# A gather queue on GpSimd: which picks wait for TensorE, and how many picks stand between the row fetches

## The chip, the cores and the metric

The kernel runs on one core of one Trainium2 chip. The metric is device time in microseconds. The kernel before has a median of 2885.0 us over three timed runs (2873.63 to 2889.99).

## The reference

One encoder layer over 1024 tokens of width 1024. A mixer sub-layer (gated linear attention and pooling) comes first; the change does not touch it. The channel sub-layer is a product-key retrieval: 8 heads choose 16 of 16384 single-neuron experts each, so 128 experts per token.

```python
def peer_ffn(h, w_q, sub_keys, u_tab, v_tab):
    q = (ht @ w_q).reshape(T, PEER_HEADS, 2, PEER_HALF)
    s = jnp.einsum('thpd,hpnd->thpn', q, sub_keys)
    vals, idx = lax.top_k(s, K)
    cand = vals[:, :, 0, :, None] + vals[:, :, 1, None, :]
    top_s, top_pos = lax.top_k(cand.reshape(T, PEER_HEADS, K * K), K)
    ...
    experts = (i1 * PEER_NKEYS + i2).reshape(T, PEER_HEADS * K)
    gates = jax.nn.softmax(top_s, axis=-1).reshape(T, PEER_HEADS * K)
    def block(args):
        a = jax.nn.gelu(jnp.einsum('td,ted->te', xb, u_tab[eb]), approximate=False)
        coeff = (gb * a.astype(jnp.float32)).astype(xb.dtype)
        return jnp.einsum('te,ted->td', coeff, v_tab[eb])
```

## The kernel before, in words

The first 1175 us hold the mixer, the queries, the scores and the first of two sweeps over the key table u. In a sweep the table is walked in 128 tiles of 128 experts (the tile number m is called a position below):

- the first key pass (m = 0 to 127) computes gelu(u . h) of every expert for the first 3 blocks of 128 tokens,
- the second key pass (m = 128 to 255) computes it for the other 5 blocks; a tile is 48 matmuls on TensorE (L1470), and every third tile is followed by 8 small ones that build the dense gates (L1964),
- the value pass (m = 256 to 383) walks the table v and adds coefficient times value row for the last 4 token blocks as a dense product; a tile is 24 matmuls of 128x512 (L1982).

The first 4 token blocks are not summed densely but gathered, on the side, during the second key pass and the value pass. For each of their 4 x 128 = 512 columns e (one chosen expert for each of 128 tokens) there are three steps:

1. a **pick**: an indirect DMA that GpSimd issues (`pick_act`, L1907), which fetches one activation per token into a column of `picked_act`,
2. a **row**: an indirect DMA that GpSimd issues (`fetch_row`, L1914), which fetches 128 rows of v, 4 KB each, into one of 7 buffers `rows`,
3. the multiply-add `ys <- rows, coef, ys` on VectorE (`add_row`, L1818). Before every eighth row VectorE forms 8 coefficients (L1809), for which the 8 picks of that group (a turn) must have landed.

GpSimd does nothing else there: its program is one fixed list of picks and rows. The order comes from `picks_by(e)`, the number of picks issued before row e. Before the change it is 13 + e, so 13 picks are ahead of row 0 and then one pick stands between two rows until all 512 are out. The list is paced: `pace(position)` makes GpSimd wait for TensorE to reach a position (through the semaphore `beats`, three marks per tile, or `tile_done`). Row e is held to `row_issue(e)`, which is 1.5 tiles ahead of where VectorE uses it in the second key pass; the pick before it has a pace of its own, half a row spacing earlier. From position 253.5 on (`2 * N - LEAD[1]`) nothing is paced any more; a row then waits only for its buffer (`rows_done`, seven rows back).

VectorE's program is in step with the tiles. At step m it does, in this order, the coefficient product of tile m + 2 (L1845, `cf`), the low half of the table tile m + 2 (`lo`, L108), the low half of the coefficients of m + 1 (`c_lo`, also named `free_hi_r`, L108), gates and top-k, and then the rows from `rows_by(m - 1)` to `rows_by(m)`: 12 rows per 5 tiles in the second key pass, 12 per 7 in the value pass. The engine works in program order, so a row that is late holds up the `lo` and `c_lo` behind it, and TensorE waits for those with `lo_ready` and `clo_ready`. In the second key pass TensorE needs from step m the `lo` of a tile two ahead; in the value pass it also needs the `c_lo` of the next tile. Rows 290 and 291 are the last of step 254; rows 292 to 294 are those of step 255. Tile 256, the first of the value pass, needs the `c_lo` of step 255, which comes behind row 291.

Of the kernel before, what the change touches and what calls it, by code (L numbers as in the profile page):

```python
# [35 lines left out]
N = NKEYS  # L36
CHOSEN = HEADS * TOPK
# [4 lines left out]
GATHERED = 4  # L42
# [33 lines left out]
POOL_ADDS = 2  # L76
ROWS_FROM, PICKS, BEATS = 133, 4, 4
ROW_EVERY = (5 / 12, 7 / 12)
PICKS_FROM, PICKS_AHEAD = N + 0.75, 12
LEAD = (1.5, 2.5)  # L80


# [1215 lines left out]
def gate_stores(s, block):  # L1298

    return len([n for n in range(block) if gate_buffer(2 * n) == s])  # L1300
# [18 lines left out]
def rows_by(m):  # L1319

    if m < ROWS_FROM:
        return 0
    late = 2 * N - 1
    rows = 12 * (min(m, late) - ROWS_FROM + 1) // 5
    return min(GATHERED * CHOSEN, rows + max(0, m - late) * 12 // 7)


def row_issue(e):

    key_rows = rows_by(2 * N - 1)  # L1330
    if e < key_rows:
        return ROWS_FROM + e * ROW_EVERY[0] - LEAD[0]
    return max(row_issue(key_rows - 1), 2 * N + (e - key_rows) * ROW_EVERY[1] - LEAD[1])


def picks_by(e):

    return min(GATHERED * CHOSEN, PICKS_AHEAD + e + 1) if e >= 0 else 0


def last_row_at(s):
# [548 lines left out]
def sweeps_gpsimd(g, pool):  # L1890

    v_table = g.i["v"].rearrange("n p d -> (n p) d")
    act_tables = [a.rearrange("n p s -> (n p s)").unsqueeze(1) for a in (g.act_early, g.act_late)]
    index = lambda a, e: a[:, e // CHOSEN, e % CHOSEN:e % CHOSEN + 1]

    def act_complete(last):
        for s in range(GELUS):
            pool.wait_ge(g.act_stored[s], 16 * ((last - s) // GELUS + 1))

    def pick_act(e):  # L1900
        turn = e // TURN
        if e == EARLY * CHOSEN:
            act_complete(2 * N - 1)
            pool.wait_ge(g.chosen_ready, 2)
        if turn >= PICKS and e % TURN == 0:
            pool.wait_ge(g.picked_in[turn % PICKS], 16 * TURN * (turn // PICKS))
        pool.indirect_dma_start(out=g.picked_act[:, e:e + 1], out_offset=None, in_=act_tables[e // (EARLY * CHOSEN)],  # L1907
                                in_offset=bass.IndirectOffsetOnAxis(ap=index(g.aidx, e), axis=0))\
            .then_inc(g.picked_in[turn % PICKS], 16)

    def fetch_row(e):
        if e >= ROWS:
            pool.wait_ge(g.rows_done, e - ROWS + 1)
        pool.indirect_dma_start(out=g.rows[e % ROWS][:], out_offset=None, in_=v_table,  # L1914
                                in_offset=bass.IndirectOffsetOnAxis(ap=index(g.eidx, e), axis=0))\
            .then_inc(g.rows_in[e % ROWS], 16)

    def pace(position):
        if position >= 2 * N - LEAD[1]:
            return  # L1920
        tile, beat = divmod(int(BEATS * min(position, 3 * N - 1)), BEATS)
        if beat:
            pool.wait_ge(g.beats, (BEATS - 1) * (tile - N) + beat)
        else:
            pool.wait_ge(g.tile_done, tile)

    pool.wait_ge(g.chosen_ready, 1)
    act_complete(N - 1)
    for e in range(GATHERED * CHOSEN):
        for p in range(picks_by(e - 1), picks_by(e)):  # L1930
            pace(PICKS_FROM + p * ROW_EVERY[0] / 2 if e == 0 else row_issue(e) - ROW_EVERY[e >= rows_by(2 * N - 1)] / 2)
            pick_act(p)
        if e == 0:
            for s in range(2):
                pool.wait_ge(g.gate_stored[s], 16 * gate_stores(s, EARLY_BLOCKS))
            pool.wait_ge(g.gate_ps, EARLY_BATCHES)
        pace(row_issue(e))
        fetch_row(e)
    for q, t in enumerate(DENSE_ORDER[:POOL_ADDS]):
        pool.wait_ge(g.y_scaled, q + 1)  # L1940
        pool.wait_ge(g.x1_dense_in, 16 * DENSE)
        pool.tensor_tensor(g.y[t][:], g.y[t][:], g.x1_dense[t][:], ALU.add).then_inc(g.y_added, 1)
# [75 lines left out]
def experts(g):  # L2018
# [3 lines left out]
    with nc.psum_tensor("sps_all", [P, 2, TT, NKEYS], F32) as sps_all, nc.Block() as block:  # L2022
# [24 lines left out]
        @block.gpsimd  # L2047
        def _(pool):
            sweeps_gpsimd(g, pool)
# [62 lines left out]
```

## Time and profile before

| | us |
|---|---|
| median of 3 timed runs | 2885.0 |
| the profiled execution, its own time | 2853.14 |
| its span, first to last instruction | 2851.3 |
| second key pass, 128 tiles | 1175 to 2114.9 |
| value pass, 128 tiles | 2114.9 to 2842.0 |

The profiled execution is shorter than all three timed ones. The mean granted TensorE clock in it is 0.997 of full. Over the span TensorE is busy 98%, VectorE 76%, ScalarE 44% and GpSimd 47%; GpSimd's share is small because it has almost nothing to do in the first 1180 us. A view lists the start and the length of a piece of work and, in brackets, how long the engine stood idle before it and what ended that.

### The profile page before, as it was taken

How to read it: one execution, taken by the hardware profiler on the slowest of the kernel's cores; microseconds unless marked ns; L12 is line 12 of the kernel's file. 1: busy time of each engine (PE TensorE's matmuls, PEld its weight loads, DVE VectorE, ACT ScalarE, POOL GpSimd, SP SyncE). 2: the span in 40 equal slices, each digit the busy share in tenths (PEclk: the TensorE clock that was granted, in tenths of full speed). 3: DMA queues.
4: the chain of work that ended last, by engine and by line, in shares of the span. 5: the costliest groups of instructions: out<-in, count | busy, mean ns of one | idle time of the engine just before them, and what ended most of it. 6: DMA issues, size and time to landing. Idle time of an engine off the chain costs nothing.

```text
span 2851.3 us, 43778 instructions
## 1 busy us (share of the span) xinstructions
PE 2783.6 (98%) x16074; PEld 2544.2 (89%) x16074; DVE 2159.0 (76%) x3706; ACT 1250.7 (44%) x2302; POOL 1341.6 (47%) x1039
## 2 busy tenths in 40 slices
PE   7998999999999999999999999999999999999998
PEld 6786788889999999999999999999997777787777
DVE  7646546887668778688888888777767877887788
ACT  4334552233367767644455535444522323232323
POOL 0002000000000000377888887777788888888884
PEclk9999999999999999999999999999999999999999
DMA  6520222225556556589898988988999999999997
GB/s 279 227 73 31 104 105 79 67 96 181 182 185 214 189 202 210 190 306 316 303 312 309 309 317 315 318 304 312 329 371 356 352 339 333 368 343 350 326 351 270
DMA packets 328418, 721.39 MB, mean 253 GB/s; under 512 B 44000, under 2 KB 159840, under 8 KB 326368
## 3 DMA queue, kind: packets, MB, share of 16 engines
q1 hardware_dynamic: 238176, 451.18, 44.9%
q0 software_dynamic: 90112, 268.76, 27.1%
q8 instruction: 47, 0.77, 0.1%
q14 instruction: 83, 0.68, 0.1%
HBM read 605.50 MB, written 114.30 MB: 252 GB/s over the span
## 4 chain that ended last, share of the span: by engine, by line
PE 56%; POOL 18%; issue 5%; DVE 2%; ACT 2%; DMA 1%; DVEq 0%; SPq 0%; ACTq 0%; POOLq 0%
PE mix L1470 44%; POOL picked_act L1907 9%; POOL rows L1914 9%; PE mix L118 5%; PE sps_all L1982 2%; PE mix L1982 2%; PE sps_all L1964 2%; DMA rows<-in_v,eidx 1%; ACT onehot L1677 1%; PE sps_all L1557 1%; DVE lo L108 0%; DVE onehot L1759 0%; DMA wq_raw<-in_w_q 0%; DVEq L1159 0%; ACT hi L103 0%
## 5 line engine op out<-in xcount | busy, mean ns | idle before, releaser
L1907 POOL DMA_INDIRECT picked_act<-act_early,aidx x384 | 491.2, 1279 | 1032.2 <-PE mix L1470 926.4
L1470 PE MATMUL mix<-a_hi,hi 128*128 128x320 f32 (+1 forms) x3072 | 809.7, 318 | 2.0 <-DVE lo L108 2.0
L1818 DVE SCALAR_TENSOR_TENSOR ys<-rows,coef,ys 128x1024 f32<-128x1024 f32 x504 | 638.4, 1286 | 228.4 <-DMA rows<-in_v,eidx 203.3
L1470 PE MATMUL mix<-a_lo,hi 128*128 128x320 f32 (+1 forms) x3072 | 808.9, 317 | 0.0
L1470 PE MATMUL mix<-a_hi,lo 128*128 128x320 f32 (+1 forms) x3072 | 808.8, 317 | 0.0
L1914 POOL DMA_INDIRECT rows<-in_v,eidx x512 | 650.9, 1271 | 164.0 <-issue 139.6
L108 DVE TENSOR_TENSOR lo<-raw,hi 128x1024 fp32r<-128x1024 f32 x384 | 468.8, 1221 | 208.8 <-ACT hi L103 208.6
L1470 PEld LDWEIGHTS mix<-a_hi,hi 128*128 128x128 f32 x3072 | 533.8, 188 | 3.3 <-ACT gelu L1686 2.3
L1470 PEld LDWEIGHTS mix<-a_hi,lo 128*128 128x128 f32 x3072 | 534.7, 188 | 0.0
L1470 PEld LDWEIGHTS mix<-a_lo,hi 128*128 128x128 f32 x3072 | 534.6, 188 | 0.0
L103 ACT ACTIVATE hi<-raw 128x1024 fp32r<-128x1024 f32 x384 | 404.7, 1054 | 290.7 <-PE mix L1982 278.9
L1689 ACT ACTIVATE gelu<-mix 128x640 f32<-128x640 f32 x128 | 90.2, 705 | 464.6 <-PE mix L1470 464.5
L1982 PE MATMUL sps_all<-hi,free_hi_r 128*128 128x512 f32 x680 | 198.4, 393 | 10.8 <-DVE free_hi_r L108 10.5
L1982 PE MATMUL mix<-hi,free_hi_r 128*128 128x512 f32 x680 | 195.5, 389 | 0.0
L1907 POOL DMA_INDIRECT picked_act<-act_late,aidx x128 | 170.9, 1335 | 39.0 <-issue 39.0
L1982 PEld LDWEIGHTS sps_all<-hi,free_hi_r 128*128 128x128 f32 x680 | 125.7, 188 | 44.9 <-DVE free_hi_r L108 19.6
L1686 ACT ACTIVATE gelu<-mix 128x384 f32<-128x384 f32 x128 | 62.8, 491 | 202.2 <-PE mix L1470 202.0
L1982 PEld LDWEIGHTS mix<-hi,free_hi_r 128*128 128x128 f32 x680 | 127.7, 188 | 26.5
L103 ACT ACTIVATE free_hi_r<-cf 128x512 fp32r<-128x512 f32 x85 | 53.6, 631 | 146.5 <-DVE cf L1845 146.3
L1982 PE MATMUL sps_all<-lo,free_hi_r 128*128 128x512 f32 x340 | 105.1, 390 | 0.0
L1982 PE MATMUL mix<-lo,free_hi_r 128*128 128x512 f32 x340 | 104.7, 389 | 0.0
L1677 ACT ACTIVATE free_hi_r<-free_hi_r,gate_hi 128x128 fp32r<-128x128 f32 x304 | 92.8, 392 | 26.6 <-DVE free_hi_r L1759 26.6
(274 smaller groups left out, 3865.0 us busy)
## 6 DMA issues: line engine op xcount, KB each, us to landing
raw<-in_u SPq DMA_DIRECT2D x256, 512.0 KB, 5.0
raw<-in_v SPq DMA_DIRECT2D x128, 512.0 KB, 5.6
act_late<-gelu SPq DMA_DIRECT2D x128, 320.0 KB, 4.7
act_in<-act_late SPq DMA_DIRECT2D x128, 256.0 KB, 6.1
act_early<-gelu SPq DMA_DIRECT2D x128, 192.0 KB, 1.8
gate_d<-free_lo SPq DMA_DIRECT2D x19, 1024.0 KB, 6.2
gt<-gate_d SPq DMA_DIRECT2D x64, 256.0 KB, 7.3
free_lo<-gate_d SPq DMA_DIRECT2D x64, 256.0 KB, 7.4
```

The source lines that it names most:

```text
L103: return act.activation(hi, raw, ACT.Copy)
L108: return dve.tensor_tensor(lo, raw, hi.bitcast(F32), ALU.subtract)
L118: done = pe.matmul(acc[:, cols], w, a[:, k, cols], start=first, stop=last)
L1470: done = pe.matmul(dst, w, a[:, k, cols], start=first, stop=last)
L1677: last = act.activation(onehot[:, t, part * NKEYS:(part + 1) * NKEYS], onehot[:, t, NKEYS:].bitcast(F32), ACT.Copy, scale=gate[:, first + ...
L1686: act.activation(g.gelu[m % GELUS][:, 0:EARLY * P], g.mps[m % 2][:, 0:EARLY * P], ACT.Gelu).then_inc(g.gelu_done, 1)
L1689: act.activation(g.gelu[m % GELUS][:].rearrange("p (a b) -> p a b", b=wide), g.mps[m % 2][:].rearrange("p (a b) -> p a b", b=HALF)[:, :, 0 ...
L1818: dve.scalar_tensor_tensor(sums, row, coef, sums, ALU.mult, ALU.add).then_inc(g.rows_done, 1)
L1907: pool.indirect_dma_start(out=g.picked_act[:, e:e + 1], out_offset=None, in_=act_tables[e // (EARLY * CHOSEN)], in_offset=bass.IndirectOff ...
L1914: pool.indirect_dma_start(out=g.rows[e % ROWS][:], out_offset=None, in_=v_table, in_offset=bass.IndirectOffsetOnAxis(ap=index(g.eidx, e), ...
L1964: last = pe.matmul(g.gps[:, t], g.onehot_1[u][:, t, :], g.onehot_2[u][:, t, :], start=True, stop=True)
L1982: done = pe.matmul(g.yps[t][:, cols], c, v[:, cols], start=n == 0 and k == 0, stop=n == N - 1 and k == 2)
```

## The change

Two things in one function and its caller: `picks_by` spreads the picks otherwise, and picks behind row 0 are no longer paced.

```diff
-PICKS_FROM, PICKS_AHEAD = N + 0.75, 12
+PICKS_FROM, PICKS_AHEAD, MORE_PICKS = N + 0.75, 12, 24
...
 def picks_by(e):
 
-    return min(GATHERED * CHOSEN, PICKS_AHEAD + e + 1) if e >= 0 else 0
+    last_key = rows_by(2 * N - 1) - 1
+    if e < 0:
+        return 0
+    if e <= last_key:
+        return PICKS_AHEAD + 1 + e + e * MORE_PICKS // last_key
+    return min(GATHERED * CHOSEN, picks_by(last_key) + (e - last_key) * 7 // 8)
...
         for p in range(picks_by(e - 1), picks_by(e)):
-            pace(PICKS_FROM + p * ROW_EVERY[0] / 2 if e == 0 else row_issue(e) - ROW_EVERY[e >= rows_by(2 * N - 1)] / 2)
+            if e == 0:
+                pace(PICKS_FROM + p * ROW_EVERY[0] / 2)
             pick_act(p)
```

`last_key` is 294: 295 rows belong to the second key pass. By the new rule 13 picks are ahead of row 0 as before, 328 are ahead of row 292 (305 before), 331 ahead of row 294 (307 before), 507 ahead of row 496 (509 before), and the last pick stands ahead of row 501 (499 before). The total is 512 picks and 512 rows in both. No other engine's list of work changes.

GpSimd in the second key pass, rows 10 to 13. Here L1907 is a pick and L1914 a row, with the semaphores that each waits for. Before:

```order
L1907 DMA picked_act<-act_early,aidx 128x1 [waits beats]
L1914 DMA rows_3624<-in_v,eidx 128x1024 [waits rows_done,beats]
L1907 DMA picked_act<-act_early,aidx 128x1 [waits beats]
L1914 DMA rows_3625<-in_v,eidx 128x1024 [waits rows_done,tile_done]
L1907 DMA picked_act<-act_early,aidx 128x1 [waits beats]
L1914 DMA rows_3626<-in_v,eidx 128x1024 [waits rows_done,beats]
L1907 DMA picked_act<-act_early,aidx 128x1 [waits beats]
L1914 DMA rows_3627<-in_v,eidx 128x1024 [waits rows_done,beats]
```

The same place now, where L1912 is a pick and L1919 a row:

```order
L1912 DMA picked_act<-act_early,aidx 128x1
L1919 DMA rows_3624<-in_v,eidx 128x1024 [waits rows_done,beats]
L1912 DMA picked_act<-act_early,aidx 128x1
L1919 DMA rows_3625<-in_v,eidx 128x1024 [waits rows_done,tile_done]
L1912 DMA picked_act<-act_early,aidx 128x1
L1919 DMA rows_3626<-in_v,eidx 128x1024 [waits rows_done,beats]
L1912 DMA picked_act<-act_early,aidx 128x1 x2
L1919 DMA rows_3627<-in_v,eidx 128x1024 [waits rows_done,beats]
```

The picks have lost their waits for TensorE's marks, the rows have kept theirs, and a second pick stands ahead of row 13; this repeats at every twelfth or thirteenth row.

GpSimd early in the value pass, rows 300 to 304. Before there is a pick between any two rows:

```order
L1914 DMA rows_3627<-in_v,eidx 128x1024 [waits rows_done]
L1907 DMA picked_act<-act_early,aidx 128x1 [waits picked_in3]
L1914 DMA rows_3621<-in_v,eidx 128x1024 [waits rows_done]
L1907 DMA picked_act<-act_early,aidx 128x1
L1914 DMA rows_3622<-in_v,eidx 128x1024 [waits rows_done]
```

And now, with one gap in every eight rows:

```order
L1912 DMA picked_act<-act_early,aidx 128x1 [waits picked_in3]
L1919 DMA rows_3623<-in_v,eidx 128x1024 [waits rows_done]
L1919 DMA rows_3624<-in_v,eidx 128x1024 [waits rows_done]
L1912 DMA picked_act<-act_early,aidx 128x1
L1919 DMA rows_3625<-in_v,eidx 128x1024 [waits rows_done]
L1912 DMA picked_act<-act_early,aidx 128x1
```

One pick in eight is missing here, since it has been issued in the second key pass.

## Rows read from the trace of the kernel before

**Rows 1.** Stretches: us, busy of PE PEld DVE ACT POOL (count), clock, DMA share, GB/s.

```profile
1175.00:2115.00 940.00, 938.80 (x6458) 938.54 (x6457) 760.13 (x1067) 439.23 (x920) 743.81 (x605) 1.00 0.89 311
2115.00:2842.00 727.00, 707.62 (x3073) 574.62 (x3071) 581.77 (x636) 219.75 (x270) 570.13 (x421) 1.00 0.95 341
```

**Rows 2.** Chain of waits, key tiles, then value tiles (start us, us, what).

```profile
2035.69 0.96 PE sps_all L1964 x8
2036.65 21.12 PE mix L1470 x144
...
2722.11 2.72 PE sps_all L1982 x12
```

**Rows 3.** The same for the inner part of the two passes.

```profile
1260.00:2100.00 840.00, 838.80 (x5772) 838.54 (x5771) 684.83 (x921) 392.50 (x822) 673.98 (x545) 1.00 0.91 315
2120.00:2780.00 660.00, 640.65 (x2779) 519.51 (x2778) 526.08 (x576) 196.83 (x236) 539.36 (x396) 1.00 0.97 347
```

**Rows 4.** Waits of GpSimd, 1260 to 2790 (total us, times, longest us).

```profile
POOL picked_act L1907 <- issue: 133.8, 439, 0.3
POOL rows L1914 <- issue: 132.6, 435, 0.3
POOL rows L1914 <- PE mix L1470: 10.4, 34, 0.3
POOL picked_act L1907 <- PE mix L1470: 9.8, 32, 0.3
```

**Rows 5.** Picks and rows: duration min/median/max in ns, first and last start.

```profile
L1907 POOL DMA_INDIRECT picked_act<-act_early,aidx x384: 942/1022/3235, 1181.5 to 2365.7; - x192
...
L1914 POOL DMA_INDIRECT rows<-in_v,eidx x512: 941/1083/3232, 1201.7 to 2814.0; - x171
```

**Rows 6.** Timeline of GpSimd, 1236 to 1253 (start, us, what, idle before).

```profile
1244.03 1.44 POOL L1914 DMA_INDIRECT rows<-in_v,eidx  x1 [1.88 <-PE mix L1470]
...
1252.18 1.24 POOL L1914 DMA_INDIRECT rows<-in_v,eidx  x1 [2.06 <-DVE ys L1818]
```

**Rows 7.** Waits of VectorE in the second key pass, then the value pass.

```profile
DVE ys L1818 <- DMA rows<-in_v,eidx: 85.2, 60, 4.0
...
DVE ys L1818 <- DMA rows<-in_v,eidx: 118.1, 98, 4.2
```

**Rows 8.** Waits of TensorE's weight loads in the value pass.

```profile
PEld sps_all L1982 <- DVE free_hi_r L108: 19.6, 24, 2.0
PEld sps_all L1982 <- DVE c_lo L108: 13.4, 12, 2.5
```

**Rows 9.** Timelines of GpSimd, VectorE and TensorE around the first value tile.

```profile
2103.93 1.09 POOL L1914 DMA_INDIRECT rows<-in_v,eidx  x1 [0.30 <-issue]
...
2108.67 1.28 DVE L1818 SCALAR_TENSOR_TENSOR ys<-rows,coef,ys 128x1024 f32<-128x1024 f32 x1 [0.28 <-DMA rows<-in_v,eidx]
2109.87 0.69 DVE L1845 TENSOR_TENSOR cf<-gt,act_in 128x512 f32<-128x512 f32 x1
2110.47 1.22 DVE L108 TENSOR_TENSOR lo<-raw,hi 128x1024 fp32r<-128x1024 f32 x1
2111.61 0.68 DVE L108 TENSOR_TENSOR c_lo<-cf,c_hi 128x512 fp32r<-128x512 f32 x1
...
2114.89 0.63 PE L1982 MATMUL sps_all<-hi,c_hi 128*128 128x512 f32 x2
```

**Rows 10.** Chain, VectorE and TensorE at TensorE's last stop for a row; last matmuls.

```profile
2703.36 6.59 DMA rows<-in_v,eidx
...
2708.58 1.28 DVE L1818 SCALAR_TENSOR_TENSOR ys<-rows,coef,ys 128x1024 f32<-128x1024 f32 x1 [2.24 <-DMA rows<-in_v,eidx]
...
2714.76 0.76 PE L1982 MATMUL sps_all<-hi,c_hi 128*128 128x512 f32 x2 [2.08 <-DVE c_lo L108]
...
2841.36 0.61 PE L1982 MATMUL mix<-hi,free_hi_r 128*128 128x512 f32 x2
```

**Rows 11.** GB/s moved in 40 slices of the span.

```profile
GB/s 279 227 73 31 104 105 79 67 96 181 182 185 214 189 202 210 190 306 316 303 312 309 309 317 315 318 304 312 329 371 356 352 339 333 368 343 350 326 351 270
```

## The prediction

> **What bounds the kernel now.** I read first the stretches by pass, then the chain of waits, then GpSimd's waits, then the timelines where the passes meet. In the second key pass TensorE is busy 938.8 of 940 us [rows 1]: the pass is TensorE's own time. The chain shows three tiles in 21.12 us and the 8 gate matmuls in 0.96 us [rows 2], so 22.08 us per three tiles, 7.36 us each. In the value pass 12 matmuls take 2.72 us [rows 2], a tile of 24 takes 5.44 us, and 128 tiles would take 696.3 us. The pass takes 727 [rows 1]: 30.7 us are lost in it. TensorE's weight loads wait there 33.0 us in 36 pieces, all for VectorE's low halves [rows 8]; those halves stand in program order behind `ys`, and VectorE waits 118.1 us for rows to land, 98 times [rows 7]. In the second key pass it also waits for rows, 85.2 us in 60 pieces, but nobody feels it [rows 1, 7].
>
> Who makes the rows late? GpSimd's share of 80% looks like slack and is none. From 1260 to 2100 it issues 545 DMAs, one per 1.541 us; from 2120 to 2780 it issues 396, one per 1.667 us [rows 3]. Between any two of them stand 0.3 us, and no single wait from 1260 to 2790 is longer: all 439 and 435 "issue" pieces are 0.3, and so are those put down to TensorE, 10.4 us in 34 and 9.8 us in 32 pieces [rows 4], which is 0.3 us each again. So the queue runs without a stop; the marks that picks and rows are held to have already gone by when it reaches them. The shortest pick and the shortest row take 0.94 us [rows 5], 1.25 us with the gap. The second key pass asks for 12 picks and 12 rows per 5 tiles, 4.8 DMAs or 7.40 us of GpSimd per 7.36 us tile; the value pass asks for 24 per 7 tiles, 3.43 DMAs or 5.71 us of GpSimd per 5.44 us tile. The first pass is level, the second is GpSimd's. The picks moved are to even this out.
>
> **Picks without their pace.** This removes waits that last nothing. Only near the start are there real ones: 1.88 us less the usual 0.3 for TensorE ahead of the row at 1244.0, and 2.06 less 0.3 for a `ys` ahead of the row at 1252.2 [rows 6], 3.3 us in all; the former is a row's own pace and stays in the code. What can be won is that more work is done before them. By row 16 one more pick has gone out (the first comes ahead of row 13), so I take 1.5 us won, between 0 and 3.3. Of the rest of this edit I take 0.
>
> **The picks that come earlier, in the second key pass.** By `picks_by`, 328 picks stand ahead of row 292 now and 305 before: 23 more. What one costs has no row of its own: issues last from 0.94 us up to 3.2 us, with medians of 1.02 and 1.08 [rows 5]. From below: it costs the shortest issue, 1.25 us [rows 5], if the time above that (1.541 - 1.25 = 0.29 us on average) is tied to what VectorE does meanwhile, of which there is no more per tile than before; 23 x 1.25 = 28.8 us. From above: the average of the stretch, 23 x 1.541 = 35.4 us. Nothing reasonable lies below zero here, as GpSimd has no idle time to put them in. Whether the time above the shortest issue follows VectorE's work, the trace doesn't say. The Trainium skill has a rule on it: its page "SBUF — State Buffer" (Who interferes with whom) says that a DMA issued by GpSimd stalls while a VectorE instruction holds the port pair that the two engines share, and that a `tensor_tensor` does not hold the part that writing descriptors needs. By the first half the low end would hold, by the second the high end, since most of VectorE's work here has two inputs like a `tensor_tensor`; no row here separates the two.
>
> I take 32 us, the middle. Rows are then late by 32 - 1.5 = 30.5 us where the passes meet. What does TensorE have to spare there? Row 292 goes out at 2103.93. The last row of step 254 is done by 2109.95 (2108.67 + 1.28); behind it come `cf`, `lo` and `c_lo`, done at 2112.29; tile 256 starts at 2114.89 [rows 9]. Its `c_lo` was ready 2.6 us early. So tile 256 starts 30.5 - 2.6 = 28 us later, near 2143 (bounds: 28.8 - 3.3 - 2.6 = 23 and 35.4 - 2.6 = 33). Most of that comes as stops of TensorE in the last third of the key pass: until the lag has used up the two-tile lead of `lo`, there is nothing to see.
>
> Behind the late rows on VectorE stand `lo`, the one-hot comparisons of the gates and top-k, and behind `lo` SP's next table load. All of them are held up by the same delay and not by one each; I cost them at nothing beyond it.
>
> **The picks that are gone from the value pass.** The last stop of TensorE for a row is at 2714.76: 2.08 us, for a `c_lo` that was behind the row issued at 2703.36 [rows 10], which is row 472 by count. From there TensorE runs to 2842.0 at its own speed. From row 292 to row 472 are 180 rows, 105 tiles, and 599.4 us. Before there are 180 picks between them, 360 DMAs at 1.665 us; now 486 - 328 = 158 picks, 338 DMAs. That is 338 x 1.665 = 562.8 us, or with the low price of a pick 599.4 - 22 x 1.25 = 571.9 us: 5.36 to 5.45 us of GpSimd per tile, against TensorE's 5.44. GpSimd is just level with TensorE, so of the 30.7 us of stops most go, and single ones stay, since the length of an issue varies from 0.94 to 3.2 us [rows 5]. I take 5 us left (0 to 15). Saved: 26 us.
>
> The sum is 28 - 26 = +2 us: 2855 us on the profiled execution's 2853.1.
>
> There is a second way to the same number, and it is the one that I trust. Ahead of row 472 stand 485 picks before and 486 now, and 472 rows in both. GpSimd never stops, so it reaches row 472 at the same time within one pick (+1.3 to +1.7) and the 1.5 us won at the start. If TensorE still waits for a row thereabouts, the end is where it was. If it doesn't, the end is set by the start of the value pass: 2143 + 696.3 = 2839, within 2834 and 2844, against 2842.0. The end is the later of the two, and with both so near each other a little more: 0 to +4. The change moves the loss from one pass to the other; it takes no work from the queue that sets the pace.
>
> The timed runs before lie 31.9 us above the profiled execution, 1.1%. Nothing shown says where. I carry the difference over unscaled: 2885 + 2 = 2887 us.
>
> **Rivals.**
> - *The value pass doesn't give the time back* (slower). TensorE's stops there would come from the transfers. For it: the pass moves 341 GB/s with the DMA engines at 0.95 [rows 1], and at 5.44 us a tile that would have to be 341 x 727 / 696 = 356 GB/s; most slices of the pass are below that. Against it: the slices also hold one of 368 GB/s in the pass and one of 371 where the passes meet [rows 11], and the row that TensorE last stopped for landed 6.59 us behind its issue [rows 10]: it was the issue that was late. Price: the key pass pays 28 us, the value pass gives between nothing and half, so +14 to +28, about +20: 2905 us. It decides where the transfers can't keep 356 GB/s over the whole pass. The Trainium skill gives such a limit: "DMA: Bandwidth & Descriptors" (Where 436 GB/s comes from) puts HBM at about 358 GB/s per core. By that page the value pass could just reach its 356 GB/s, with nothing over for unevenness. The trace's slice of 371 speaks against a limit below that.
> - *The key pass has room* (faster). In the profile GpSimd is level with TensorE (7.40 to 7.36 us). If in the timed runs the 31.9 us extra are mostly TensorE's or VectorE's, GpSimd would have up to that much room before the passes meet, would be held by its paces, and the 23 early picks would cost little there while the value pass still gives 26. It would be -15 to -26, about -20: 2865 us. Against it: nothing in the profile shows such room; the waits of 0.3 us say the opposite.
> - *The change doesn't do what it says*: the free picks have no idle time to go into. That is part of my forecast for the pace; for the order of picks it isn't so, since the list is fixed by the program.
>
> **How the numbers follow.** The forecast has 60%, the slower rival 23%, the faster one 14%; the other 3% I leave open. Within 0.5% (14 us) is what a measurement of this kernel can't tell from no change. My own terms leave it only at their far ends: 33 us in the key pass and 15 left in the value pass give +17, 23 and 0 give -8. So of the 60, 54 are same, 4 slower, 2 faster; of the rivals, 4 of the 23 and 3 of the 14 fall inside 0.5%. With the rest split this gives faster 0.14, same 0.62, slower 0.24. The likeliest case alone reaches from 2877 to 2902; with the rivals, and the spread of 16 us that the runs before show, the range is 2866 to 2909.
>
> **What would show it.** In the profile after: GpSimd's waits from 1260 to 2790 still all 0.3 us; the DMAs issued per us in either pass as before; TensorE with stops of 20 to 30 us in the last third of the second key pass, with VectorE's `lo` (or the one-hots) as what it waits for; the first value tile near 2143; a value pass of about 701 us instead of 727, and VectorE's waits for rows there well below 118 us. I am wrong if tile 256 starts before 2130 (the key pass had room, or a pick costs less than the shortest issue), if GpSimd shows waits of over 0.3 us for TensorE along the key pass, or if the value pass stays above 715 us with GpSimd no longer late.

## The result, and the profile after

The changed kernel took 2892.84 us, the median of 22 runs (2879.96 to 2915.84), against 2878.62 us for the kernel before (22 runs, 2869.20 to 2891.15, the three shown above among them): a ratio of 1.0051, interval 1.0037 to 1.0065. The forecast was 2887 us and +2, within 2866 to 2909; the time is within its range, and the difference is +14.

The profiled execution took 2892.82 us, at the median of the timed runs; that of the kernel before took 2853.14, below all of its own. So of the 39.7 us between the two traces about 26 are not shown by the timed runs, which differ by 14.

The stretches by pass after the change, with the columns of [rows 1]:

```profile
1176.00:2184.00 1008.00, 971.79 (x6456) 956.64 (x6455) 759.21 (x1068) 440.55 (x920) 752.50 (x635) 0.98 0.86 292
2184.00:2880.00 696.00, 696.00 (x3073) 576.40 (x3072) 580.28 (x636) 208.20 (x268) 542.15 (x391) 1.00 0.97 353
```

Against [rows 1] the key pass is 68 us longer, where 28 were forecast, and the value pass 31 us shorter, without any stop of TensorE. The key pass has lost in two columns: 36 us in which TensorE is idle, and a clock of 0.98 (2% of 1008 us is 20 us).

What ended the idle time of TensorE's weight loads in the key pass, then the same for VectorE and its rows (engine, what, releaser: total us, times, longest us):

```profile
PEld mix L1475 <- issue: 48.0, 77, 1.9
PEld sps_all L1970 <- issue: 2.2, 5, 0.5
```

```profile
DVE ys L1823 <- DMA rows<-in_v,eidx: 7.7, 8, 2.6
```

This is not what was forecast. The stops stand inside key tiles, in 77 short pieces, and wait for nothing that the profile shows; and VectorE waits 7.7 us for rows where it waited 85.2 [rows 7]. TensorE's timeline at the first of them (start us, us, what, idle before):

```profile
1299.16 0.31 PE L1475 MATMUL mix<-a_lo,hi 128*128 128x320 f32 x1
1300.03 0.40 PE L1475 MATMUL mix<-a_lo,hi 128*128 128x320 f32 x1 [0.56 <-issue]
1300.74 0.31 PE L1475 MATMUL mix<-a_hi,lo 128*128 128x320 f32 x1 [0.31 <-issue]
1301.46 0.30 PE L1475 MATMUL mix<-a_hi,lo 128*128 128x320 f32 x1 [0.41 <-issue]
1302.87 0.45 PE L1475 MATMUL mix<-a_hi,hi 128*128 128x320 f32 x2 [1.10 <-issue]
```

Matmuls that elsewhere follow one another every 0.15 us come 0.7 to 1.4 us apart, one by one, in the middle of a tile whose operands are all there. Two windows of TensorE (us, busy and count, clock, DMA share, GB/s), one over such an episode and one between two of them:

```profile
1480.00:1495.00 15.00, 10.95 (x50) 0.66 0.86 280
1502.00:1545.00 43.00, 43.00 (x298) 1.00 0.85 294
```

There are some 15 such episodes from 1300 to 2168 (pieces less than 12 us apart taken as one), none in the value pass. Beside or behind eight of them the clock is granted at 0.5, the 1.2 GHz level, for 3.4 to 10.2 us: 44.4 us in all, which costs 22. With the 36 us of idle time that is 58 of the 68 us. The other 10 are in the busy column too, since a matmul that stands alone counts 0.3 to 0.4 us where one in a row takes 0.15. GpSimd, in the meantime (1260 to 2720), had time over:

```profile
POOL picked_act L1912 <- issue: 135.3, 444, 0.3
POOL rows L1919 <- issue: 118.9, 390, 0.3
POOL rows L1919 <- remote: 33.6, 20, 2.7
POOL rows L1919 <- DVE ys L1823: 18.7, 15, 4.0
POOL rows L1919 <- PE mix L1475: 17.7, 24, 1.8
```

Three groups of waits are longer than the 0.3 us of [rows 4]: GpSimd is held by TensorE's marks, by `ys`, and by something that the profile doesn't name (`remote`). TensorE lost its time first and thereby gave the queue the room that it lacks in the trace before. So this trace can't show what the moved picks cost. It took experiments.

### The profile page after: what moved, and what is told of

It reads as the page before. It is cut to its first block, busy times and chain, and to the rows that moved or that the text cites. A ratio compares the mean times of both kernels' runs of the same rounds, so it can differ in the third digit from the quotient of the medians.

```text
span 2891.0 us, 43743 instructions
## 1 busy us (share of the span) xinstructions
PE 2807.3 (97%) x16074; PEld 2566.0 (89%) x16074; DVE 2157.3 (75%) x3706; ACT 1241.4 (43%) x2302; POOL 1322.8 (46%) x1039
## 3 DMA queue, kind: packets, MB, share of 16 engines
q1 hardware_dynamic: 238176, 451.18, 44.4%
q0 software_dynamic: 90112, 268.76, 27.2%
## 4 chain that ended last, share of the span: by engine, by line
PE 80%; DVE 2%; issue 2%; ACT 1%; DVEq 0%; DMA 0%; SPq 0%; ACTq 0%
PE mix L1475 48%; PE sps_all L1988 12%; PE mix L1988 12%; PE mix L118 5%; PE sps_all L1970 2%; ACT onehot L1682 1%; PE sps_all L1562 1%; DVE lo L108 0%; DVE onehot L1764 0%; DMA wq_raw<-in_w_q 0%; DVEq L1159 0%; ACT hi L103 0%; DVE rows L1887 0%; DVE idx L1178 0%; DVE idx L1167 0%
## 5 line engine op out<-in xcount | busy, mean ns | idle before, releaser
L1912 POOL DMA_INDIRECT picked_act<-act_early,aidx x384 | 474.0, 1234 | 1032.9 <-PE mix L1475 914.6
L1475 PE MATMUL mix<-a_lo,hi 128*128 128x320 f32 (+1 forms) x3072 | 819.6, 320 | 14.1 <-issue 14.0
L1475 PE MATMUL mix<-a_hi,hi 128*128 128x320 f32 (+1 forms) x3072 | 818.4, 320 | 13.0 <-issue 10.7
L1475 PE MATMUL mix<-a_hi,lo 128*128 128x320 f32 (+1 forms) x3072 | 817.1, 320 | 9.9 <-issue 9.6
L1919 POOL DMA_INDIRECT rows<-in_v,eidx x512 | 644.1, 1258 | 219.9 <-issue 136.5
L1823 DVE SCALAR_TENSOR_TENSOR ys<-rows,coef,ys 128x1024 f32<-128x1024 f32 x504 | 628.1, 1283 | 13.8 <-DMA rows<-in_v,eidx 7.7
L1475 PEld LDWEIGHTS mix<-a_lo,hi 128*128 128x128 f32 x3072 | 541.2, 190 | 21.3 <-issue 20.9
L1475 PEld LDWEIGHTS mix<-a_hi,lo 128*128 128x128 f32 x3072 | 540.7, 190 | 12.2 <-issue 12.1
L1912 POOL DMA_INDIRECT picked_act<-act_late,aidx x128 | 176.1, 1376 | 39.0 <-issue 39.0
L1682 ACT ACTIVATE free_hi_r<-free_hi_r,gate_hi 128x128 fp32r<-128x128 f32 x304 | 93.0, 394 | 1.4 <-DVE free_hi_r L1764 1.3
```

The lines of the kernel that those rows point to most:

```text
L1475: done = pe.matmul(dst, w, a[:, k, cols], start=first, stop=last)
L1682: last = act.activation(onehot[:, t, part * NKEYS:(part + 1) * NKEYS], onehot[:, t, NKEYS:].bitcast(F32), ACT.Copy, scale=gate[:, first + ...
L1823: dve.scalar_tensor_tensor(sums, row, coef, sums, ALU.mult, ALU.add).then_inc(g.rows_done, 1)
```

## The experiments

They ran in three sets on two other chips (called the other chips below), where the kernel before takes 2842 to 2844 us (2841.83, 2843.66 and 2842.08 in the sets, 19 to 28 runs each). The first and the third set are of one chip; the second (`more_48`, `more_12`, `half_picks`, `early_rows`) is of the other and holds no profile of the two kernels unedited. A ratio is to the kernel before in the same set. No profile there shows an episode inside a tile.

**The kernel before and the kernel after, unedited**, each profiled twice (the second pair in the last set, to see how far two executions of one kernel differ).

> The kernel before, profiled once more. Theory Q (the queue: TensorE loses time only to late rows): a second key pass of 940 us with no stop of TensorE inside a tile, a value pass of about 727 us, 2853 us in all. Theory S (TensorE starves inside tiles of the second key pass, in episodes that no wait explains, each followed by a stretch at the lower clock; the first profile of the kernel before happened to hold none): a second key pass of 955 to 990 us with such episodes, and a value pass nearer 700 us since GpSimd catches up during them; about 2875 us, the level of the other timed runs of this kernel.

> The changed kernel, once more, timed in five rounds. Both theories: ratio 1.003 to 1.007. Theory Q: a second key pass of about 968 us and a value pass of about 700 us. Theory S: a second key pass of 990 to 1015 us, of which all above 940 us stands in pauses inside tiles and in halved clock after them; value pass 697 us.

> The kernel before, one more look, for the stops of TensorE inside tiles that no wait explains (15 episodes in the first profile of the changed kernel, none in the two profiles of this one). If they belong to the chip and not to the change, and this is the chip on which the kernel before takes about 2880 us, they are here too: clock below 0.993 and a second key pass above 955 us. On a chip where it takes about 2842 us: none, 939 and 720 us.

> The changed kernel, one more look, for the same stops. On a chip where the kernel before takes about 2842 us: no episodes inside tiles, key pass 955 to 960 us, value pass 697 to 706 us. On the one where it takes about 2880 us: episodes again, key pass about 1000 us. If there are episodes here and none in the look at the kernel before, they go with the change (theory S2).

Measured: before 2843.51 and 2842.44 in the two profiled executions; after 2848.18 over its timed runs (the profiled one 2851.48), 1.0028 [1.0012, 1.0045], and 2846.47 in the second look. Stretches by pass, before (two looks), then after (two looks):

```profile
1175.40:2114.10 938.70, 938.55 (x6457) 938.29 (x6456) 759.11 (x1067) 439.05 (x920) 741.42 (x609) 1.00 0.90 312
2114.10:2832.40 718.30, 704.68 (x3073) 575.63 (x3072) 583.86 (x637) 217.52 (x270) 562.75 (x417) 1.00 0.96 344
```

```profile
2118.50:2831.30 712.80, 702.16 (x3074) 574.78 (x3072) 582.40 (x636) 217.56 (x270) 558.96 (x415) 1.00 0.96 345
```

```profile
1176.80:2134.00 957.20, 946.00 (x6457) 942.84 (x6455) 758.30 (x1066) 438.75 (x920) 756.58 (x625) 0.99 0.88 305
2134.00:2839.00 705.00, 699.03 (x3072) 578.29 (x3072) 583.10 (x638) 208.44 (x269) 550.87 (x401) 1.00 0.97 352
```

```profile
1178.10:2137.70 959.60, 944.06 (x6457) 940.81 (x6456) 760.75 (x1067) 438.66 (x920) 757.72 (x629) 1.00 0.88 305
2137.70:2834.20 696.50, 696.48 (x3073) 576.36 (x3072) 582.60 (x636) 212.21 (x270) 548.16 (x397) 1.00 0.97 355
```

This is the trade that was forecast, smaller on both sides: the key pass gives 18.5 to 19.6 us, the value pass gets 13 to 16 back. Behind the value pass the span is another 1.2 to 1.4 us longer (10.7 and 10.5 us, against 9.3 twice before). GpSimd's waits in the first look after the change, from 1260 to row 472 at 2694:

```profile
POOL picked_act L1912 <- issue: 137.2, 450, 0.3
POOL rows L1919 <- issue: 129.2, 424, 0.3
POOL rows L1919 <- PE mix L1475: 7.0, 23, 0.3
```

Not one is longer than 0.3, nor in the second look. Row 472 goes out at 2694.0 and 2693.9 after the change, at 2694.4 and 2690.3 before it. What ended TensorE's stops (weight loads), and what the one-hots waited for on ScalarE, key pass:

```profile
PEld sps_all L1970 <- issue: 8.6, 8, 2.7
PEld mix L1475 <- DVE lo L108: 4.1, 2, 3.8
...
ACT free_hi_r L1682 <- DVE free_hi_r L1764: 122.9, 24, 7.7
```

The gate matmuls, which follow every third tile, are where the late rows show first: VectorE's comparisons (L1764) stand behind `ys`, ScalarE's weighing (L1682) behind them, the gate matmuls (L1970) behind that. Before the change ScalarE waits there for 23.6 and 32.3 us in the two looks, in 7 and 8 pieces.

Where the passes meet, TensorE and VectorE of the same trace:

```profile
2133.94 0.69 PE L1988 MATMUL sps_all<-hi,c_hi 128*128 128x512 f32 x2
...
2141.91 1.28 DVE L1823 SCALAR_TENSOR_TENSOR ys<-rows,coef,ys 128x1024 f32<-128x1024 f32 x1 [5.65 <-DMA rows<-in_v,eidx]
...
2144.86 0.68 DVE L108 TENSOR_TENSOR free_hi_r<-cf,free_hi_r 128x512 fp32r<-128x512 f32 x1
...
2145.59 1.22 PE L1988 MATMUL sps_all<-hi,free_hi_r 128*128 128x512 f32 x2 [5.97 <-DVE free_hi_r L108]
```

One row, 5.65 us late, holds `ys`, behind it `cf` and the low half, and TensorE for 5.97 us in its second value tile. After that it doesn't stop again. The row is row 294, and the last of the 24 early picks stands right ahead of it: from row 293 GpSimd goes through two picks, and row 294 goes out 8.0 us behind row 292, against 5.0 in both looks before. In the second look after it is 7.1 us, the row lands three us earlier, and TensorE has no stop there at all.

**The two halves apart.** The picks without their pace, in the old order; and the new order with the pace restored:

```diff
# unpaced_only, on the kernel before
-            pace(PICKS_FROM + p * ROW_EVERY[0] / 2 if e == 0 else row_issue(e) - ...)
+            if e == 0:
+                pace(PICKS_FROM + p * ROW_EVERY[0] / 2)
# order_only, on the kernel after: the reverse of this
```

> Only the pace of the picks behind row 0 is taken away; the order of picks and rows is that of the kernel before. Theory Q: nothing was waited for, so ratio 1.000 (within 0.002), at most 1.5 us faster. Theory S1 (picks without their waits bring the episodes): ratio 1.005, as the whole change, more episodes in the second key pass than the kernel before has, value pass 697 to 727 us.

> Only the new order of picks (24 more in the second key pass, seven per eight rows in the value pass); each pick keeps its pace. Theory Q: the same as the whole change, 1.005, since the waits were empty. Theory S1: ratio 1.000 or below, few episodes. Theory S2 (more picks in the second key pass bring the episodes, waits or not): 1.005.

Measured: unpaced_only 2846.7 us, 1.0019 [1.0004, 1.0034]; order_only 2848.22 us, 1.0024 [1.0007, 1.0041]. The key pass of each:

```profile
1182.20:2120.50 938.30, 938.30 (x6457) 938.30 (x6456) 759.27 (x1068) 439.50 (x920) 740.46 (x610) 1.00 0.91 313
```

```profile
1177.80:2138.40 960.60, 945.20 (x6456) 941.93 (x6455) 759.11 (x1066) 438.93 (x920) 759.37 (x627) 0.99 0.88 304
```

The order alone brings 20.6 to 21.9 us in the key pass, the pace none of it. By their times the two halves can't be told apart. The interval of unpaced_only just excludes 1.0000, and its trace doesn't show why: the passes take 938.3 and 712.9 us, as before, and the 3.7 to 6.8 us by which it is late are there at the start of the key pass (1182.2, against 1175.4 and 1178.5), ahead of the edit. That its 1.0019 is a loss by the pace is not shown.

**The dose.** Twice and half as many early picks, the value pass relaxed to match:

```diff
# more_48, on the kernel after
-... MORE_PICKS = N + 0.75, 12, 24
+... MORE_PICKS = N + 0.75, 12, 48
-    ... + (e - last_key) * 7 // 8)
+    ... + (e - last_key) * 6 // 8)
# more_12: 12, and * 15 // 16
```

> Twice the dose: 48 picks more in the second key pass instead of 24, and six picks per eight rows after it; no pace on the picks. 47 picks more than before stand ahead of row 292, 3 more ahead of row 472. Theory Q with the low price (a moved pick costs the shortest issue, 1.25 us): row 292 goes out 57 us later than before, the first value tile starts 48 us later (+30 over the changed kernel), the key pass is 987 to 995 us with halved clock after each stop, the value pass is 696 us with no stop at all; ratio 1.010 to 1.013. With the high price (1.54 us) row 292 is 72 us late and the ratio 1.016 to 1.018. Theory W (only what TensorE waits for counts, and the one-hots are no nearer to their limit than now): ratio 1.003, as now.

> Half the dose: 12 picks more in the second key pass and fifteen per sixteen rows after it; no pace on the picks. 11 picks more than before ahead of row 292, none more ahead of row 472. Theory Q: row 292 is 12 us late, which the room of VectorE where the passes meet takes up for the most part: key pass 939 to 945 us, value pass 710 to 715 us; row 472 goes out when it did, so ratio 1.000 to 1.002. Theory W (it pays to move some picks, and 24 were too many): 0.997.

Measured: more_48 2871.6 us, 1.0085 [1.0054, 1.0116]; more_12 2843.1 us, 0.9999 [0.9981, 1.0017]. By pass, more_48:

```profile
1179.40:2156.40 977.00, 948.50 (x6457) 943.86 (x6455) 759.02 (x1065) 440.82 (x923) 771.34 (x648) 0.99 0.87 299
2156.40:2862.20 705.80, 701.12 (x3072) 579.53 (x3072) 584.23 (x638) 206.42 (x267) 513.76 (x378) 0.99 0.97 351
```

Its key pass is 37 to 38 us longer than before, its value pass only 7 to 12 us shorter. No trace has a value pass below 696.0, and the picks moved beyond what that takes win nothing: GpSimd now waits 59.1 us in it for `ys` to free a row's buffer. The 9 us above 696.5 are one stop of 4.68 us at its start and the lower clock. So the loss grows with the picks moved (0.9999, 1.0028, 1.0085), and it does so on chips that show no stops inside tiles. The profile of more_12 (2850.6 us of span, 953.8 us in the key pass) is 9 us over its own median once the 1.8 us around the span are added; it shows stops in the key pass that its expectation did not have.

**Without half of the picks.** Every second pick is left out, with its data (the activations that it would bring stay at zero):

```diff
# half_picks, on the kernel before
 def pick_act(e):
+    if e % 2: return
...
-    wait_ge(picked_in, 16 * TURN * ...)
+    wait_ge(picked_in, 16 * TURN // 2 * ...)
```

> Leaves out every second pick (the columns stay zero, so the gathered sums lack half their terms); rows, order and paces as before. 768 issues on GpSimd instead of 1024. Theory Q: the queue has room and is held by its paces, the stops of TensorE in the value pass go (22 to 31 us): key pass 939 us, value pass 696 to 698 us, GpSimd with waits of over 0.3 us for TensorE all along; ratio 0.990 to 0.992. Rival T (the transfers bound the value pass): it stays above 710 us, since the bytes are the same.

Measured: 2826.4 us, 0.9932 [0.9911, 0.9953]. Its stretches, and GpSimd's waits from 1260 to 2790:

```profile
1176.20:2114.50 938.30, 938.30 (x6457) 938.30 (x6456) 755.04 (x1068) 438.73 (x920) 562.07 (x456) 1.00 0.90 313
2114.50:2811.00 696.50, 696.48 (x3073) 576.38 (x3072) 581.38 (x636) 208.66 (x270) 426.98 (x314) 1.00 0.97 353
```

```profile
POOL rows L1917 <- DVE ys L1819: 211.9, 106, 4.8
POOL rows L1917 <- PE mix L1470: 174.9, 121, 4.4
```

With GpSimd's load reduced it waits for its marks and for `ys`, as it hardly ever does before, and TensorE runs both passes without a stop. So what the queue costs the kernel before is about these 19 us, in the value pass. That no order of picks can win more follows if TensorE's own time stays as it is; it was not tested otherwise.

**Rows earlier.** The first row a tile earlier, all rows of the key pass due a tile earlier, and no pace on any pick; with 0, 24 and 12 early picks:

```diff
# early_rows on the kernel before; early_24 and early_12 on after and more_12
-ROWS_FROM, PICKS, BEATS = 133, 4, 4
+ROWS_FROM, PICKS, BEATS = 132, 4, 4
-LEAD = (1.5, 2.5)
+LEAD = (2.5, 2.5)
-            pace(...)          # before pick_act(p)
```

> The order of before, no pace on any pick (the first 13 included), rows from tile 132 instead of 133 and paced 2.5 tiles ahead instead of 1.5: the queue starts its rows 4 us earlier and loses none of the 5.6 us that it stands still before 1253. Theory Q: everything behind is 8 to 10 us earlier in the queue, so row 472 too, and the end by as much, since TensorE still waits for rows in the value pass: key pass 939, value pass 708 to 712 us, ratio 0.997. Theory W: the start is far from where TensorE waits, ratio 1.000.

> The changed kernel's order of picks, with the early start of the rows (rows from tile 132, paced 2.5 tiles ahead, no pick paced). The early start put row 292 12 us earlier after the start of the second key pass, the new order puts it 27 us later: 15 us in all. Theory Q: VectorE's room takes 9 of these, so the stops and halved clock of the second key pass fall from 18 us to 5 to 8, the value pass runs at TensorE's pace (697 to 700 us): ratio 0.994 to 0.996, faster than the kernel before and than the changed one. Theory W (moving picks earlier is bad whatever the start): 1.002.

> The same early start with half the dose of early picks (12, then fifteen per sixteen rows). Theory Q: row 292 about where it was before, no stop of TensorE in the second key pass, 939 us; the value pass keeps some stops (705 to 709 us against 718): ratio 0.995 to 0.997. Theory W: 1.000.

Measured: early_rows 2839.9 us, 0.9983 [0.9967, 0.9999]; early_24 2846.86 us, 1.0013 [1.0000, 1.0027]; early_12 2833.93 us, 0.9964 [0.9950, 0.9979]. The stretches of early_12, and TensorE at its one long stop:

```profile
1177.10:2124.70 947.60, 941.17 (x6456) 940.91 (x6456) 761.74 (x1071) 439.15 (x920) 749.42 (x625) 0.99 0.90 311
2124.70:2821.20 696.50, 696.50 (x3074) 576.88 (x3072) 578.54 (x633) 208.79 (x270) 536.75 (x401) 1.00 0.96 352
```

```profile
1623.76 2.07 PE L1968 MATMUL sps_all<-free_hi_r 128*128 128x256 f32 x8 [6.43 <-ACT free_hi_r L1682]
```

early_12 is faster than both kernels. The queue starts earlier and half as many picks are moved: the value pass runs at 696.5, and the key pass loses 8 to 9 us in place of 19. The early start alone (early_rows, 0.9983) does little: row 472 goes out at 2688.7, 2 to 6 us earlier than in the two looks at the kernel before, and the value pass still takes 713.9. What is left in early_12 is nearly all at one place, 6.43 us for the weighed one-hots ahead of the gate matmuls in tile 188, and the slower clock behind it (10.2 us). early_24 is a miss: 0.994 to 0.996 was expected. Its profiled execution, 2832.73 us, is the lowest of its 12 runs (up to 2853.35) and shows what was expected, 947.1 and 697.4 us by pass, so that one trace must not be read as the kernel. Why the other runs are slower is open.

## Why the prediction was right, and where it wasn't

*What was luck.* The time fell within the range on the first chips, but the one trace of the change there doesn't show the forecast's mechanism. It shows one of its signs of being wrong, GpSimd waiting for TensorE along the key pass, 17.7 us in pieces of up to 1.8. The +14 there is at the far end of what the forecast's own terms give (+17), and the stops that made most of that trace's loss were in no term. What bears the mechanism out is the other chips, where the measured difference is +6.

*The queue never stops: right on the other chips.* All waits of GpSimd in the stretch stay at 0.3 us, and row 472 goes out at the same time as before within the spread of two looks (2693.9 and 2694.0 to 2690.3 and 2694.4). The loss moved from one pass to the other, as the second way to the number had it.

*Unpaced picks worth 1.5 us (0 to 3.3): no gain in time.* In unpaced_only's trace row 292 goes out 919.1 us behind the first key tile, against 922.5 and 920.9, which is about the size forecast and hardly more than two looks differ; its timed runs gain nothing.

*23 picks ahead of row 292 cost 32 us: too much.* From the first tile of the key pass to row 292 it takes 922.5 and 920.9 us before, and 949.6, 947.3 and 949.9 in after_again, after_again_2 and order_only: 27.2 us more on average, 1.18 us a pick. That is a little under the low end of 1.25, not the middle. 47 picks in more_48 took 48.7 us more, 1.04 each; the 11 in more_12's single trace took 23.8, 2.2 each, so that one trace of such a kernel is not enough to price a pick (both are of the chip without a profile of the kernel before, and are held against the looks on the other). The mean per DMA from the pass's start to row 292 fell from 1.545 and 1.543 us before (597 DMAs) to 1.532 and 1.528 after (620) and 1.507 in more_48 (644). So a moved pick costs about the shortest issue, and the time above it doesn't grow with the number of picks. Of the Trainium skill's rule in "SBUF — State Buffer" (Who interferes with whom), weighed in the prediction, this speaks for the first half, that a GpSimd DMA is stretched by VectorE's work. It does not show it: no run here changed VectorE's work alone.

*Tile 256 28 us later: 19 to 20, and once 25 with the stop behind it.* After against before, the key pass is 18.5 us longer in the first pair, and TensorE then stops 5.97 us in tile 257; in the second pair it is 19.6 us longer, and no stop follows. Row 292 is 27.1 and 26.4 us late in its pass, so 8.6 and 6.8 us of that were taken up, where the forecast allowed 2.6. The 2.6 are right for the trace they were read from. On the other chips the queue was further ahead before the change, with row 292 at 922.5 and 920.9 us of the pass instead of 928.9, and VectorE stood still there for the high half of a table tile (9.10 and 7.02 us) and not for rows.

*"TensorE stops in the last third of the key pass": wrong place.* The step left out that the one-hots of the gates stand in the same queue on VectorE and are due after every third tile, with ScalarE's weighing still to come behind them. In both looks TensorE stops from tile 176 on (the pass is tiles 128 to 255), with 8 of the 23 early picks out, and for these one-hots first. The trace before the change has one such stop already, 1.2 us at 1748. In after_again_2:

```profile
1530.47 1.21 PE L1970 MATMUL sps_all<-free_hi_r 128*128 128x256 f32 x8 [0.48 <-ACT free_hi_r L1682]
```

The first long stop of after_again, at tile 188, waits for the low half behind them:

```profile
1624.48 0.56 PE L1475 MATMUL mix<-a_hi,hi 128*128 128x320 f32 x2 [3.56 <-DVE lo L108]
```

"I cost them at nothing beyond it" was said of just these comparisons.

*The clock: a term that the sum lacked.* Behind that stop of 3.56 us, and around and behind the one of 5.97 us, stands a stretch at the lower clock. Windows of after_again, with full clock in between (us, busy and count of PE, PEld, DVE, ACT, POOL, clock, DMA share, GB/s):

```profile
1625.10:1628.50 3.40, 3.40 (x15) 3.40 (x14) 3.33 (x7) 0.56 (x1) 2.78 (x3) 0.50 1.00 396
1640.00:1660.00 20.00, 20.00 (x140) 20.00 (x139) 16.11 (x30) 9.76 (x21) 15.51 (x14) 1.00 0.84 288
2143.90:2150.70 6.80, 5.11 (x12) 4.04 (x13) 6.76 (x9) 2.14 (x3) 5.58 (x5) 0.50 1.05 398
```

In that trace the 1.2 GHz level holds for 10.2 us of the key pass and 6.8 of the value pass and costs up to half of that, 8.5 us; in the profile of [rows 1] it is 3.4 us, and 1.7 lost. The 30 us of stops of the kernel before are spread over 36 pieces, the longest 2.5 us [rows 8]; the change makes few and longer ones out of many short ones. By trace, the lower clock holds in the two passes together for 3.4 and 0 us in the looks before, 17.0 and 6.8 after and 10.2 in order_only. Half of that, the most that it can cost, is 6.8 and 3.4 us more in the two pairs, and the two passes together are 5.2 and 3.3 us longer: without the clock the trade would have been about even. How much of the +6 of the timed runs is the clock's is not shown. Their mean granted clock (0.996 in the median before, 0.994 after, but 0.995 in both order_only and unpaced_only) also holds the first 1175 us, where the lower clock takes 10 to 31 us whatever the edit.

*The value pass 727 to 701: right in size after, better before.* It is 705.0 and 696.5 us after, but 718.3 and 712.8 before on that chip. So it gave 13 to 16 us and not 26.

*The rivals.* That transfers hold the value pass is dropped: it ran in 696.5 us at 355 GB/s. For most of it, in after_again, it was even more:

```profile
2140.00:2780.00 640.00, 634.41 (x2788) 525.26 (x2789) 532.19 (x582) 187.40 (x238) 524.18 (x381) 0.99 1.00 363
```

The Trainium skill gives about 358 GB/s of HBM per core, as half of what the two cores of a stack share ("DMA: Bandwidth & Descriptors", Where 436 GB/s comes from). This trace, of a kernel on one core, moves 363 GB/s for 640 us and 396 and 398 in the short windows above, so if these bytes are counted as the page counts them, 358 was no limit here. That the key pass has room was true of the profile after, but as an effect of TensorE's stops, and it won nothing.

*Left open.* On the first chips the change cost 14 us and not 6. The 15 episodes inside tiles cost 68 us in the one trace, and they are in none of the 13 others. The kernel before has none in its trace, but its timed runs lie 25 us above that trace, so it may have them too, fewer or shorter; no trace shows it. All 22 runs after the change have a mean clock of 0.984 to 0.992 against 0.990 to 0.996 for the same kernel in its first set on the other chips; that fits with episodes in all of them and doesn't prove it. That they came with the unpaced or with the early picks was a theory in the expectations; on the other chips neither order_only, unpaced_only nor more_48 brings any. It wasn't tried on the first chips. That about 8 of the 14 us are theirs is argued, not shown.

## What to carry to other kernels

When a queue issues without a stop, moving work within it moves the loss and doesn't remove it: find the item whose lateness is felt last, count what stands ahead of it in either order, and expect the end where it was, plus what the lower clock takes behind the stops. Count also what else stands behind the late item on its engine, with its own due time: here it was the one-hots, not `lo`, that TensorE missed first. What helps such a queue is less work in it (0.9932 without half of the picks) or an earlier start (0.9964 with a tile's start and 12 early picks; with 24 it gave 1.0013, for a reason that is open). Take at least two traces of a kernel before pricing a few us from them: those of early_24 and more_12 each told another story than the medians did.

## What the runs showed of the hardware

- An indirect DMA holds GpSimd for at least 0.94 us, with 0.30 us to the next, whether it brings 128 x 1 or 128 x 1024 elements [rows 5]; extra ones in a full queue added 1.0 to 1.2 us each (one trace: 2.2).
- TensorE worked at the 1.2 GHz level for 3.4 us behind a stop of 3.56 us and for 6.8 us around and behind one of 5.97 us (rows above); in `after_again` 3.4 us each also stand at stops of 2.46 and 2.27 us, and in the trace before the change at one of 2.08 us.
- TensorE can stop inside a tile with all operands there: 77 pieces of up to 1.9 us in one trace of one chip, none in any trace of another. Its cause is not known.
